# A block of two layers on one core: x multiplied out before its norm, the gate chain ahead, and keys times the state subtracted from the values before T

## The reference, cut to what matters

```python
hn = rmsnorm(h, norm_mix_g)                     # row root times h times gain
qkv, gate, a_raw, b_raw = split(hn @ w_in)
qkv = silu(causal_dwconv(qkv, conv_w))          # four taps
g = -exp(a_log) * softplus(a_raw + dt_bias); beta = sigmoid(b_raw)
G = cumsum(g, over the chunk)
tri = strict_lower(beta * k k^T * decay) + I    # T is its inverse
u, w = T (v * beta), T (k * beta * exp(G))
v_new = u - w S;  o = (q exp(G)) S + (q k^T * decay) v_new
S = chunk_decay * S + k_dec^T v_new
out = rmsnorm(o) * silu(gate) @ w_out
```

## Time and profile before

| | |
|---|---|
| median of 3 runs | 1437.5 us (1435.81 to 1437.81) |
| profiled execution: its own time | 1436.72 us |
| its span, first to last instruction | 1434.9 us |
| PE busy | 1391.0 us, 97% of the span |
| VectorE busy | 748.4 us, 52% |
| ScalarE busy | 606.9 us, 42% |
| GpSimd busy | 24.3 us, all in the first 37 us |
| DMA queues together | 86 GB/s over the span |

### The profile page before, as it was taken

The page is one execution under the profiler, slowest core; times in us unless marked ns, Lnnn a source line. Parts: engine busy times, 40 slices in busy tenths (PEclk is TensorE's granted clock), DMA queues, the critical chain, the costliest instruction groups (busy, mean ns, idle before and its releaser), DMA issues.

```text
span 1434.9 us, 18557 instructions
## 1 busy us (share of the span) xinstructions
PE 1391.0 (97%) x6729; PEld 1139.5 (79%) x6729; DVE 748.4 (52%) x1088; ACT 606.9 (42%) x961; POOL 24.3 (2%) x19
## 2 busy tenths in 40 slices
PE   6599999999989999999999999999999999999998
PEld 3488888888768888888887777777888888888886
DVE  7667666666464334343456543447643343434555
ACT  4446555655444223142346445544442232323342
POOL 6000000000000000000000000000000000000000
PEclk9799999999999999999999999999999999999999
DMA  4222322312133333333233312112433333333323
GB/s 148 59 60 60 73 59 73 60 52 63 63 90 101 103 88 103 101 90 102 88 91 120 115 57 59 44 54 65 161 95 105 95 103 88 92 103 96 88 88 103
DMA packets 42338, 124.09 MB, mean 86 GB/s; under 512 B 3952, under 2 KB 12720, under 8 KB 41776
## 3 DMA queue, kind: packets, MB, share of 16 engines
q1 hardware_dynamic: 33472, 117.08, 27.2%
q10 hardware_dynamic: 8816, 6.33, 2.5%
HBM read 119.17 MB, written 4.23 MB: 86 GB/s over the span
## 4 chain that ended last, share of the span: by engine, by line
PE 92%; DVE 3%; ACT 2%; DMA 1%; issue 1%; POOL 1%; SPq 0%; ACTq 0%; DVEq 0%; POOLq 0%
PE acc L306 26%; PE acc L308 25%; PE acc L307 25%; PE ps L421 2%; PE ps L443 2%; PE ps L643 2%; PE ps L627 1%; PE ps L659 1%; DVE work L1333 1%; POOL work L1265 1%; PE ps L401 1%; DMA work<-rows 1%; DVE wl L281 1%; PE ps L671 0%; PE ps L464 0%
## 5 line engine op out<-in xcount | busy, mean ns | idle before, releaser
L306 PE MATMUL acc<-xh,wh 128*128 128x512 f32 x976 | 401.8, 412 | 0.0
L308 PE MATMUL acc<-xh,wl 128*128 128x512 f32 x976 | 381.5, 391 | 0.0
L307 PE MATMUL acc<-xl,wh 128*128 128x512 f32 x976 | 380.7, 390 | 0.0
L275 ACT ACTIVATE wh<-raw 128x1024 fp32r<-128x1024 f32 x208 | 217.4, 1050 | 179.4 <-DMA raw<-in_weights 152.3
L281 DVE TENSOR_TENSOR wl<-raw,wh 128x1024 fp32r<-128x1024 f32 x208 | 254.6, 1224 | 71.2 <-ACT wh L275 68.0
L306 PE MATMUL acc<-yh,wh 128*128 128x512 f32 x656 | 259.8, 396 | 19.0 <-DVE yl L1786 12.0
L308 PE MATMUL acc<-yh,wl 128*128 128x512 f32 x656 | 257.3, 392 | 0.0
L307 PE MATMUL acc<-yl,wh 128*128 128x512 f32 x656 | 257.3, 392 | 0.0
L308 PEld LDWEIGHTS acc<-xh,wl 128*128 128x128 f32 x976 | 183.3, 188 | 39.7
L306 PEld LDWEIGHTS acc<-xh,wh 128*128 128x128 f32 x976 | 184.1, 189 | 37.6 <-issue 4.9
L307 PEld LDWEIGHTS acc<-xl,wh 128*128 128x128 f32 x976 | 184.0, 189 | 35.7 <-issue 4.1
(11 more groups left out here) (239 smaller groups left out, 1207.4 us busy)
## 6 DMA issues: line engine op xcount, KB each, us to landing
raw<-in_weights SPq DMA_DIRECT2D x208, 512.0 KB, 3.5
work<-rows ACTq DMA_DIRECT2D x16, 256.0 KB, 6.8
h<-in_xT SPq DMA_DIRECT2D x4, 512.0 KB, 6.6
proj<-work ACTq DMA_DIRECT2D x2, 1024.0 KB, 4.2
work<-proj SPq DMA_DIRECT2D x2, 1024.0 KB, 7.4
outT<-h SPq DMA_DIRECT2D x8, 256.0 KB, 2.5
cst<-in_cst SPq DMA_DIRECT2D x1, 640.0 KB, 4.0
work<-in_pT SPq DMA_DIRECT2D x1, 512.0 KB, 5.9
```

What stands on the lines that cost most here:

```text
L275: nc.scalar.activation(wh[u.const % 4][:], raw[u.const % 2][:], ACT.Copy).then_inc(hi_done, 1)
L306: nc.tensor.matmul(dst[:], hi, mh[:, k, :], start=(n == 0), stop=False)
L307: nc.tensor.matmul(dst[:], hi, ml[:, k, :], start=False, stop=False)
L308: mm = nc.tensor.matmul(dst[:], lo, mh[:, k, :], start=False, stop=(n == KT - 1))
```

## The change

It has three parts.

1. xh, xl are x times the gain, without the root, for all heads; yh, yl and GpSimd's work in turn 0 are gone. The root stays in `xrstd` and VectorE multiplies every unit of every head by it as it leaves PSUM (`take`, `take_gate`). Before, ScalarE emptied the banks of turns 1 to 8 with two copies per unit, of which the second was the first tap. Now ScalarE has the first tap alone, from `xpad` (`first_tap`), in turn 0 too. VectorE adds the squares.
2. In turn 0 the gate steps stand ahead of the taps, the rows are fetched before the value taps, and turn 1 begins with six unit steps before x(1) (`FIRST_FILL`).
3. `w`, its negated copy and the scaled keys are gone. `ks(c)` multiplies the kept keys (`kcur`) by S, `correct(c)` on VectorE adds that, scaled by a table that now has its sign turned, to the values vb, and v(c) is T times these, one matmul where two added up before.

```diff
                     last.then_inc(tx_d, 1)
                 return step

-            def w():
-                pe.wait_ge(tt_d, i * 6)
-                for c in range(1, C):
-                    last = nc.tensor.matmul(ch(ps[1], c), ch(kb, c), ch(TT, c), start=True, stop=True)
-                last.then_inc(w_d, 1)
-                if project:
-                    pe_ktr(pe, i)
+            def ks(c):
+                def step():
+                    if c == 1:
+                        pe.wait_ge(kcur_d, i)
+                    pe.wait_ge(s_d, b * 3 + c)
+                    nc.tensor.matmul(ch(ps[3], c), ch(kcur, c), S, start=True, stop=True).then_inc(ks_d, 1)
+                    if c == 1:
+                        pe.wait_ge(qd_d, i)
+                    nc.tensor.matmul(ch(ps[5], c), S, ch(qd, c), start=True, stop=False)
+                return step

             def v(c):
                 def step():
                     if c == 0:
+                        pe.wait_ge(tt_d, i * 6)
                         pe.wait_ge(vb_d, i)
-                    last = nc.tensor.matmul(ch(ps[3], c), ch(TT, c), ch(vb, c), start=True, stop=(c == 0))
-                    if c > 0:
-                        if c == 1:
-                            pe.wait_ge(nw_d, i)
-                        pe.wait_ge(s_d, b * 3 + c)
-                        last = nc.tensor.matmul(ch(ps[3], c), ch(nw, c), S, start=False, stop=True)
-                    last.then_inc(v_d, 1)
-                    if c > 0:
-                        if c == 1:
-                            pe.wait_ge(qd_d, i)
-                        nc.tensor.matmul(ch(ps[5], c), S, ch(qd, c), start=True, stop=False)
+                    else:
+                        pe.wait_ge(v0_d, b * 3 + c)
...

             return ([x(1), tx(1), vtr] + [s for n in range(2, 7) for s in (x(n), tx(n))]
-                    + [w] + [s for c in range(C) for s in (v(c), os(c))] + ([] if project else [norm]))
-
-        FILL = [2, 2, 0, 2, 2, 2, 2, 2, 2, 2, 2, 2, 1, 1, 1, 1, 1, 1, 1, 1, 1, 1]
-        assert sum(FILL) == 4 * KT
+                    + [v(0), os(0)] + [s for c in range(1, C) for s in (ks(c), v(c), os(c))] + ([] if project else [norm]))
+
+        FILL = [0, 2, 2, 0, 2, 2, 2, 2, 2, 2, 2, 1, 2, 1, 0, 1, 1, 1, 1, 1, 1, 1, 1, 1, 1]
+        FIRST_FILL = [6, 2, 2, 0, 1, 2, 1, 2, 1, 2, 1, 1, 1, 1, 0, 1, 1, 1, 1, 1, 1, 1, 1, 1, 0]
+        assert sum(FILL) == sum(FIRST_FILL) == 4 * KT

         OUT_AHEAD = ((4, 5), (5,), (5,), (), (), (), (2,), (2,))
-        LAST_FILL = [1, 1, 0, 1, 1, 1, 1, 1, 1, 2, 2, 1, 1, 1, 1, 1, 1, 1, 1, 1, 1, 2, 4]
...
-                        for _ in range(FILL[at]):
+                        for _ in range(fill[at + 1]):
                             next(todo)
                     else:
                         for _ in range(LAST_FILL[at]):
...
-                gates = dict(zip((8, 13, 22, 27), pe_gate_steps(pe)))
+                gates = dict(zip((8, 12, 17, 21), pe_gate_steps(pe)))
                 for n in range(4 * KT):
                     if n in gates:
                         gates[n]()
-                    next(todo)
...
-            def take(n):
+            def first_tap(n):
...
-                nc.scalar.activation(xpad[:, 3:3 + T], acc[u.const % 2][:], ACT.Copy)
+                act.wait_ge(evac[u.const % 2], u.half(1))
                 act.wait_ge(cwc_d, i + 1)
...
+                if head and n == 2:
                     act.wait_ge(vtr_d, i)
                 tap = (1, 0, 2)[n] * TAPS + 3
...
                 nc.scalar.activation(buf, buf, ACT.Silu).then_inc(done, 1)

             if not head:
                 s1, s2, s3 = act_gate_steps(act)
-                split_hi(act, Unit(2))
                 act.wait_ge(g_pe, 1)
                 split_hi(act, Unit(3))
-                normed(0, 3)
                 s1()
+                first_tap(0)
+                s2()
                 split_hi(act, Unit(4))
-                s2()
-                normed(3, KT)
+                s3()
+                first_tap(1)
                 silu(kc, 3, k_silu)
+                act.wait_ge(g_dma, 16)
+                act_rows(act, 0)
                 silu(qc, 6, q_silu)
-                s3()
-                act.wait_ge(xl_done, KT)
                 act_ksq(act, 0)
+                first_tap(2)
                 silu(vc, 9, v_silu)
                 act.preload_act_table_set(LN_EXP)
-                act.wait_ge(g_dma, 16)
-                act_rows(act, 0)
                 act_decay(act, 0)
                 nc.scalar.activation(eg, grow, ACT.Exp).then_inc(eg_d, 1)
...
+            def take(n):
+
+                u = Unit(n, i, 4)
+                dve.wait_ge(unit_done, u.number(1))
+                if n > 0 or head:
+                    dve.wait_ge(conv_st, i * 9 + 3 * n)
+                if n > 0 or head:
+                    dve.wait_ge(tap3_d, i * 3 + n)
+                nc.vector.tensor_tensor(xpad[:, 3:3 + T], acc[u.const % 2][:], xrstd, ALU.mult).then_inc(evac[u.const % 2], 1)
+
+            def take_gate():
+
+                u = Unit(-1, i, 4)
+                dve.wait_ge(unit_done, u.number(1))
+                if past:
+                    dve.wait_ge(g_silu, b)
+                nc.vector.tensor_tensor(graw, acc[1][:], xrstd, ALU.mult).then_inc(evac[1], 1)
...
-                s1, s2, s3 = dve_gate_steps(dve)
-                nc.vector.tensor_copy(cwc.unsqueeze(2), cwall[:, :, bass.ds(i, 1)]).then_inc(cwc_d, 1)
+                s1, s2a, s2b, s2c, s3 = dve_gate_steps(dve)
+                k_taps, q_taps, v_taps = (conv_steps(n) for n in range(3))
+                s1()
                 take(0)
-                s1()
+                s2a()
+                next(k_taps)
+                s2b()
+                next(k_taps)
+                s2c()
+                next(k_taps)
+                s3()
+                split_lo(dve, Unit(3))
                 take(1)
-                s2()
                 nc.vector.tensor_copy(tcg.unsqueeze(2), tab5[:, 0:C, bass.ds(i, 1)]).then_inc(tcg_d, 1)
-                normed(0, 3)
+                for _ in q_taps:
+                    pass
+                split_lo(dve, Unit(4))
                 take(2)
-                s3()
-                normed(3, KT)
-                dve.wait_ge(unit_done, 4)
-                nc.vector.tensor_tensor(graw, acc[1][:], W(20), ALU.mult).then_inc(evac[1], 1)
-                nc.vector.tensor_copy(c3(TT0), over_chunks(ident)).then_inc(id_d, 1)
+                for _ in v_taps:
+                    pass
                 next_knorm()
                 next_beta()
...
             x_mask(1)
             split_lo(dve, Unit(1, i, 4))
             upd(1)
+            take_gate()
+            x_mask(2)
             if past:
                 dve_osum(dve, b)
-            x_mask(2)
...
             x_mask(3)
             if project:
-                next(k_taps)
-                next(k_taps)
+                take(0)
+            if past:
+                dve_o1(dve, b)
             upd(3)
             if project:
                 next(k_taps)
             x_mask(4)
-            if past:
-                dve_output(dve, b)
+            if project:
+                next(k_taps)
+                next(k_taps)
             upd(4)
             if past:
+                dve_yb(dve, b)
+            x_mask(5)
+            if project:
+                take(1)
+            else:
+                split_lo(dve, Unit(U_OUT1 + 2))
+            if past:
                 dve_yl(dve, b)
-            x_mask(5)
+            upd(5)
             if project:
                 next(q_taps)
                 next(q_taps)
-            else:
-                split_lo(dve, Unit(U_OUT1 + 2))
-            upd(5)
-            if project:
                 next(q_taps)
                 split_lo(dve, Unit(3, i, 4))
-                next_beta()
             else:
                 split_lo(dve, Unit(U_OUT1 + 3))
             upd(6)
             if project:
+                next_beta()
                 next_mask()
                 next_knorm()
...
+            def correct(c):
+                dve.wait_ge(ks_d, b * 3 + c)
+                if c == 1:
+                    dve.wait_ge(vb_d, i)
+                nc.vector.scalar_tensor_tensor(out=ch(vb, c), in0=ch(ps[3], c), scalar=tc(2, c), in1=ch(vb, c),
+                                               op0=ALU.mult, op1=ALU.add).then_inc(v0_d, 1)
             state(0)
+            correct(1)
             if project:
+                take(2)
                 next_pairs()
                 split_lo(dve, Unit(4, i, 4))
             state(1)
+            correct(2)
             if project:
                 next_ti()
                 next(v_taps)
             state(2)
+            correct(3)
             if project:
                 next(v_taps)
                 next(v_taps)
...
             split_lo(dve, Unit(1))
+            nc.vector.tensor_copy(cwc.unsqueeze(2), cwall[:, :, bass.ds(0, 1)]).then_inc(cwc_d, 1)
```

(18 more changed lines are left out.)

139 lines of the change are left out of this document (48 added, 91 removed).

## The result

The changed kernel takes 1446.8 us (median of 4 runs, 1446.25 to 1448.1) against 1436.8 for the kernel before (4 runs, 1435.81 to 1437.81). The ratio is 1.007, 95% interval 1.0058 to 1.0082: slower by 10.0 us, where 4.9 were forecast. The profiled execution took 1446.8 us with a span of 1445.0, 10.1 longer than the span of before.

The account below looks back on a forecast made before the run. PE, busy 97% of the span, was taken to bound the kernel; -14.1 (turn 0) + 0.3 (turn 1) + 0.8 + 16.3 (turns 2 to 7) + 1.6 (turn 8) = +4.9 us gave 1442 us, range 1433.5 to 1449.

Parts of the forecast that it names:

- the two waits that make most of the loss: Turns of the loop: PE waits 1.24 us for the norm's sum in x(2) and 1.1 us for state(1) at ks(2).
- the likeliest case: Whole kernel: the forecast's own case, 1442 us with a range of 1440 to 1446; chance 40%.
- Turn 0: Start to x(1) of turn 1: x(1) starts at 53.1 us, 14.1 earlier than before.
- The main step: Turn 0: with GpSimd silent, PE meets no late low part from VectorE; unit 0 ends at 16.0 us, before at 21.07.
- the rows' trip: Turn 0: fetched near 37.4 us, rows land near 45.3, with 1.6 us of margin before the decay.
- Turn 1: First turn of the loop: +0.3 us, 42.1 long against 41.85, with waits of 4.75 in all.
- rival C: Loop turns: one stop a turn brings a half-clock stretch, 1.7 x 6 = 10 us more, 1452 us; chance 10%.
- The norm's wait: x(2) in turns 2 to 8: PE waits 1.24 us for VectorE's sum, plus 0.1 on the next matmul, 1.34.
- ks(2): Tail of turns 2 to 7: VectorE needs 3.2 us from take(2) to state(1), PE 2.06, so PE waits 1.1.
- The small waits: Turns 2 to 7: v(0) 0.2, os(0) 0.3, ks(1) 0.1, 0.6 us together, plus 0.35 of restarts.
- Turn 8 to the end: Last turn: norm's wait stays, no take, w gone, x_mask a little later: +1.6 us; the rest unchanged.
- B (the cover holds in the tail): Loop tail: only the norm's 1.34 less 0.66 remains, +0.7 us a turn; 1430 us in all; chance 18%.

Follow-up runs that it names:

- experiment 1: Changed kernel with the output norm's sum moved ahead of take_gate and x_mask(2) in VectorE's queue; 1439.6 us, ratio to the kernel before 1.002.
- Experiment 3: Changed kernel with take_gate of turn 1 ahead of x_mask(1) instead of behind upd(1); 1445.1 us, ratio to the kernel before 1.005.
- experiment 2: Changed kernel with VectorE's tail reordered: pairs ahead of correct(1), take(2) behind the low part; 1437.7 us, ratio to the kernel before 1.0004.
- experiment 11: Kernel before and changed kernel run once more each, unchanged, to read the clock at the MLP border; 1436.4 and 1448.2 us.
- experiment 6: Kernel before with part 3 alone, ScalarE's emptying of bank 0 behind the copy of v(1); 1439.6 us, ratio to the kernel before 1.0026.
- experiment 10: Changed kernel with sum, take(2) and turn 1's take_gate reordered, eight steps ahead of x(1), and w back (part 3 undone); 1421.9 us, ratio to before 0.99.

## Why the prediction was right, and where its sum was off

The sign, and 1446.8 inside the range, were right, and so were the two waits that make most of the loss. But the forecast of 1442 was 4.8 low, outside the likeliest case's own 1440 to 1446, and the loss measured, 10.0 us, is about twice the one forecast. By its own steps:

- **Turn 0**, -14.1 forecast, -13.5 measured. Unit 0 ended at 17.0, not 16.0: I let the clock rise in the third step as before, but it rose in the fifth (a matmul takes 0.63 up to the one at 13.59). That is the run's and not the kernel's: in experiment 1, which has the same turn 0, it rose in the third, unit 0 ended at 15.3, and x(1) started at 52.15, where the forecast had 53.1 and this profile 53.75. The main step held: VectorE's low parts take 0.70 each where they took 1.63 beside GpSimd's adds (2.81 for the four from 10.95 on, below), and PE waits for none of them. That GpSimd's silence is the reason fits these rows, and no experiment tested it alone. The gate chain was not late, the rows' trip had margin, and the decay followed the table load (predicted 46.9, found 47.6). The wait of 5.8 for Ti, forecast "under 8", is there.

```profile
10.95 2.81 DVE L1776 SCALAR_TENSOR_TENSOR xl<-h,par,xh 128x512 fp32r<-128x512 f32 x4 [0.35 <-ACT xh L1199]
```

- **Turn 1**, +0.3 forecast, +3.3 measured: the largest single miss. The wait for `take_gate` was sized well (1.9 for 2.1), and those at tx(6) and the transposes roughly (0.9 for 1.2, 0.5 for 0.6); the tail's only one with a bracket is ks(2)'s 0.2. Most of what was missing is the clock: a granted 0.57 from 62 to 66 us behind that wait, 1.7 us, and x(1) to tx(1) with both steps between them wholly at 0.50, where before it was 0.60, 0.7 us. These are 2.4 of the 3.0 us; the other 0.6 no experiment placed. I had the first at hand as the mechanism of rival C and priced it only for the loop. Experiment 3 shows it: without the wait, no stretch and 3.8 us less.
- **The norm's wait**, 1.24 + 0.1 forecast: 1.19 in the bracket, 2.25 - 0.90 = 1.35 in all. Shown by experiment 1.
- **ks(2)**, 1.1 forecast: 1.04 in the bracket, 2.36 - 1.14 = 1.22 with its start. That `take(2)` begins late and everything behind it follows in a chain is in the rows to 0.05 us, and experiment 2 shows that the order in the tail is the cause.
- **The small waits**, 0.6 + 0.35 of starts forecast, 1.3 found: a turn costs 3.25 + 0.66 = 3.9 in waits, of which 1.35 and 1.22 are the two above. v(0) waits the 0.2 forecast; the step that I had not seen is the transposes at L382, which wait for ScalarE's silu of the keys once w no longer stands ahead of them (0.2). That made a turn +3.25 in place of +2.7, 2.8 us over five turns.
- **Turn 8 to the end**, +1.6 forecast, 0.0 measured. Up to the MLP it is there: the first matmul of L306 behind the wait for h starts 46.45 us after x(1) before and 47.99 after, 1.5 more. It is given back behind the second wait for h, where the first profile of before has its stretch at half clock (0.66 over 5 us, 1.7 us lost) and that of the changed kernel has none. That is luck: in experiment 11 it falls the other way in both kernels, and the changed one takes 1448.2.
- **Rivals.** B (the cover holds in the tail) is refuted by ks(2)'s row. C did not happen in the loop: the granted clock is 1.00 in turn 4, with several stops in each. It did happen in turn 1, behind 1.93 us. The rule of the Trainium skill (TensorE: Matmul & The Clock Gate, Part 1), that the clock falls only after idleness that goes on, fits the waits of 1.0 to 1.2 us of the loop, behind which none fell, and does not fit turn 1 nor the fall behind 1.6 us in the earlier trace rows; the same part also tells of a kernel whose short stops between groups of matmuls made the clock go back and forth. What I held against C, the wait of 1.9 us that no stretch follows, does not hold either: in experiment 6's profile the same wait, 1.97 us up to 33.48, is followed by a granted clock of 0.50 from 35 to 37 us.

Against the change as a whole: part 1 and the earlier gate steps are worth 13.5 us, and were spent by two instructions put ahead of the wrong one in VectorE's queue. Part 3 takes work off the engine that bounds the kernel and still loses by 0.3 to 0.5 us a turn in the orders that were tried (experiments 6 and 10), and the rows show where it goes: os(0), ks(1) and, with part 1, v(0) and the transposes come to PE before ScalarE or VectorE is done with what they need, while w needed nothing that was late. That the longer chain from one state to the next (a correction more) adds to it was only argued.

## What to carry to other kernels

When work moves to an engine that has time to spare, read its queue and not its load: the question for each inserted instruction is what stands behind it and who waits for that, and whether the inserted one has itself to wait. An emptying of a bank waits for the bound engine's latest work, so put it behind everything that this engine will ask for next; the same emptying in the way cost 1.2 us a turn on VectorE and 1.1 on ScalarE. The limit is the next unit for that bank: in turn 1 an emptying that came too late cost PE 1.9 us and a stretch at half clock besides. And matmuls removed from an engine without waits are a gain only where what follows them is ready earlier too.

## What the runs showed of the hardware that was not expected

- At the border to the MLP the same instructions come out 1.6 to 2.6 us apart from run to run. From the first matmul behind PE's second wait for h to the end of the span, eight of the fourteen profiles take 1015.9 to 1016.0 us; the other six, in which a stretch at half clock stands there, take 1017.5 to 1018.6. The length of the wait does not tell which: behind 3.4 us it did not fall (the changed kernel's first profile), behind 1.8 it did (its second). That is enough to hide or feign an effect of this size between two single profiles.
- The half-clock stretch between the two waits for h cost nothing in experiment 11, since the wait behind it was shorter by as much (1.7 in place of 3.3 us, and 1.8 in place of 3.4). A mean clock over a long window counts such a stretch too: from 400 to 450 us it is 0.97 in both profiles of the kernel before, of which one loses 1.6 us there and the other nothing.
- Behind a stop, even one too short to have a bracket, the first matmul itself takes longer: 0.33 us to the next in place of 0.22 at ks(2) (226.71 to L458 at 227.04), and as much at ks(1), which has no bracket. No list of waits shows these; only the distances between instructions do.
